# Grouping the tile shapes of a gated recurrence's score and output matmuls

## The reference, cut to what matters

```python
def chunk_gated_recurrence(q, k, v, log_f):
    C = HGRN_CHUNK                       # 64
    ...
    b = jnp.cumsum(lf, axis=-2)
    b_mid = b[..., C // 2:C // 2 + 1, :]
    scores = jnp.einsum('nbhtk,nbhsk->nbhts', q * jnp.exp(b - b_mid), k * jnp.exp(b_mid - b))
    o_intra = jnp.einsum('nbhts,nbhsv->nbhtv', jnp.where(causal, scores, 0.0), v)
    q_inter = q * jnp.exp(b)
    k_state = k * jnp.exp(b_last - b)
    def step(state, xs):
        qi, ks, vc, dec = xs
        o = jnp.einsum('bhtk,bhkv->bhtv', qi, state)
        state = dec[..., None] * state + jnp.einsum('bhsk,bhsv->bhkv', ks, vc)
        return state, o
    ...
    o = o_intra + o_inter
```

## Time and profile before

| | value |
|---|---|
| median of three runs | 1926.18 us (1922.85 to 1926.97) |
| span of the profiled execution, first to last instruction | 1922.8 us (the page gives no other time for it) |
| PE busy | 1847.2 us, 96% of the span |
| DVE busy | 1548.3 us, 81% |
| ACT busy | 1237.2 us, 64% |
| mean DMA rate | 256 GB/s |
| mean granted TensorE clock | 0.983 of full |

### The profile page before, as it was taken

How to read it: one execution, slowest core, us unless ns; L and a number is a source line. 1 busy time by engine, 2 the same in 40 slices (tenths; PEclk the granted TensorE clock), 3 DMA queues, 4 the chain that set the end, 5 groups by cost and what they waited for, 6 DMA issues and landing times.

```text
span 1922.8 us, 26965 instructions
## 1 busy us (share of the span) xinstructions
PE 1847.2 (96%) x9968; PEld 1576.8 (82%) x9968; DVE 1548.3 (81%) x1597; ACT 1237.2 (64%) x1280; POOL 1.4 (0%) x6
## 2 busy tenths in 40 slices
PE   7888999998899999999899999999999999999998
PEld 7777899887689988876788888888878888788886
DVE  8965788476567755665999998999989899898997
ACT  6966655366544435553577776777767777677776
POOL 0000000000000000000000000000000000000000
PEclk9999999999899999999899999999999999999999
DMA  9422455543135554433499998999989999899995
GB/s 369 148 88 88 162 189 176 197 154 110 66 142 187 178 195 154 140 117 127 177 380 361 356 376 323 373 364 362 382 313 366 370 369 373 330 355 375 350 377 207
DMA packets 68369, 491.48 MB, mean 256 GB/s; under 512 B 7712, under 2 KB 8096, under 8 KB 8992
## 3 DMA queue, kind: packets, MB, share of 16 engines
q1 hardware_dynamic: 67968, 488.52, 67.3%
q0 software_dynamic: 288, 1.31, 0.2%
HBM read 488.75 MB, written 1.05 MB: 255 GB/s over the span
## 4 chain that ended last, share of the span: by engine, by line
PE 84%; DVE 8%; ACT 5%; issue 2%; DMA 0%; SPq 0%; DVEq 0%; ACTq 0%
PE ps L419 25%; PE ps L428 19%; PE ps L421 19%; PE ps L430 6%; PE ps L423 6%; DVE wl L3076 1%; DVE wl L2126 1%; PE ps L439 1%; ACT wh L1423 1%; PE ps L1242 1%; PE ps L1340 1%; PE ps L1061 1%; DVE hTl L2184 1%; PE ps L1098 1%; PE ps L834 1%
## 5 line engine op out<-in xcount | busy, mean ns | idle before, releaser
L3076 DVE TENSOR_TENSOR wl<-raw,wh 128x2048 fp32r<-128x2048 f32 x336 | 760.9, 2288 | 57.4 <-ACT wh L2060 52.5
L2060 ACT ACTIVATE wh<-raw 128x2048 fp32r<-128x2048 f32 x336 | 644.3, 1919 | 205.9 <-PE ps L428 205.9
L419 PE MATMUL ps<-wh,hTh 128*128 128x512 f32 (+2 forms) x1128 | 444.5, 395 | 10.6 <-issue 5.1
L421 PE MATMUL ps<-wh,hTl 128*128 128x512 f32 (+2 forms) x1128 | 435.5, 387 | 0.0
L2126 DVE TENSOR_TENSOR wl<-raw,wh 128x2048 fp32r<-128x2048 f32 x124 | 283.6, 2290 | 125.0 <-ACT wh L1423 124.7
L1423 ACT ACTIVATE wh<-raw 128x2048 fp32r<-128x2048 f32 x125 | 238.5, 1913 | 138.1 <-PE ps L428 70.2
L428 PE MATMUL ps<-wl,hTh 128*128 128x512 f32 (+2 forms) x1128 | 301.4, 386 | 0.0
L419 PEld LDWEIGHTS ps<-wh,hTh 128*128 128x128 f32 x1128 | 212.7, 189 | 55.5 <-issue 11.0
L419 PE MATMUL ps<-wh,work_r 128*128 128x512 f32 x648 | 255.2, 394 | 0.4 <-DVE work_r L3081 0.4
L421 PE MATMUL ps<-wh,work_r 128*128 128x512 f32 x648 | 253.0, 390 | 0.0
L421 PEld LDWEIGHTS ps<-wh,hTl 128*128 128x128 f32 x1128 | 212.8, 189 | 40.2
(11 more groups left out here) (430 smaller groups left out, 1634.4 us busy)
## 6 DMA issues: line engine op xcount, KB each, us to landing
raw<-in_units SPq DMA_DIRECT2D x461, 1024.0 KB, 7.1
x<-in_x SPq DMA_DIRECT2D x2, 512.0 KB, 5.0
work<-in_lru_w SPq DMA_DIRECT2D x1, 1024.0 KB, 14.5
xn<-in_mem SPq DMA_DIRECT2D x1, 1024.0 KB, 17.5
out<-x SPq DMA_DIRECT2D x2, 512.0 KB, 3.1
consts<-in_consts POOLq DMA_DIRECT2D x1, 768.0 KB, 4.5
xn<-in_moe_gain POOLq DMA_DIRECT2D x1, 512.0 KB, 5.8
consts<-in_consts SPq DMA_DIRECT2D x1, 352.0 KB, 10.9
```

The source lines that it names most:

```text
L419: nc.tensor.matmul(out, sh, mh, start=(first and j == 0), stop=False)
L421: nc.tensor.matmul(out, sl, mh, start=False, stop=False)
L2060: A(wh[:, n % SPLIT, :], raw[:, n % RAW, :], ACT.Copy).then_inc(sem("hi_made"), 1)
L3076: V.tensor_tensor(wl[:, n % SPLIT, :], raw[:, n % RAW, :], wh[:, n % SPLIT, :].bitcast(F32), ALU.subtract).then_inc(sem("lo_made"), 1)
```

## The change

Nothing is computed otherwise; only the order of calls, two waits and the start flags differ. In `hg_scores` the loop over the two shapes is now the outermost: eight calls of 32 columns, then eight of 64. In `hg_out_of` the four score products come first and then the four state products, and the two waits for the state products stand between the two groups. Since two heads share a bank, only the first of them clears it (`start=(h % 2 == 0)`).

```diff
-            for h in (2 * pair, 2 * pair + 1):
-                for c in range(4):
-                    q0 = 64 * (c % 2)
-                    for m, lo in ((32, 0), (64, 32)):
+            for m, lo in ((32, 0), (64, 32)):
+                for h in (2 * pair, 2 * pair + 1):
+                    for c in range(4):
+                        q0 = 64 * (c % 2)
                         col0 = h * P + (c // 2) * 64 + lo
                         ins = nc.tensor.matmul(ps[q0:q0 + m, 4, col0:col0 + 32], gK[:, h, c * 64:c * 64 + m],
                                                gQ[:, h, c * 64 + lo:c * 64 + lo + 32], start=True, stop=True)
...
+            o = [ps[q0:q0 + 64, 6 + h // 2, (h % 2) * S + t * P:(h % 2) * S + (t + 1) * P] for h in range(4)]
+            for h in range(4):
+                ins = nc.tensor.matmul(o[h], AT[q0:q0 + 64, h, t * 64:(t + 1) * 64], gv[half][q0:q0 + 64, t, h * P:(h + 1) * P],
+                                       start=(h % 2 == 0), stop=(c == 0), skip_group_check=True)
             if c > 0:
                 pe.wait_ge(*reached("hgrn_factors", 4 * half + 3))
                 pe.wait_ge(*reached("hgrn_state", 3 * half + c))
-            for h in range(4):
-                o = ps[q0:q0 + 64, 6 + h // 2, (h % 2) * S + t * P:(h % 2) * S + (t + 1) * P]
-                ins = nc.tensor.matmul(o, AT[q0:q0 + 64, h, t * 64:(t + 1) * 64], gv[half][q0:q0 + 64, t, h * P:(h + 1) * P],
-                                       start=True, stop=(c == 0))
-                if c > 0:
-                    ins = nc.tensor.matmul(o, gq[:, 4 * half + h, c * 64:(c + 1) * 64], state[(c - 1) % 2][:, h, :], start=False,
-                                           stop=True)
+                for h in range(4):
+                    ins = nc.tensor.matmul(o[h], gq[:, 4 * half + h, c * 64:(c + 1) * 64], state[(c - 1) % 2][:, h, :],
+                                           start=False, stop=True, skip_group_check=True)
             counted(ins, "hgrn_o")
```

## The result

The changed kernel's first four executions took 1909.63 us in the median (1909.35 to 1916.81), against 1924.62 for the kernel before (1922.85 to 1926.97, four executions); the ratio is 0.9927 with a 95% interval of 0.9912 to 0.9942. Two later measurements of the same changed kernel gave 1913.88 and 1914.05 us, ratios 0.9943 [0.9925, 0.9960] and 0.9936 [0.9923, 0.9948].

A forecast was written before the change was run, and what follows sets the result against it. PE was taken to bound the recurrence layer; stretches capped by two waits gave 3.5 + 0.84 + 3.4 + 2.5 = 10.3 us, so 1926.18 - 10.3 = 1915.9 us. The range was 1911.8 to 1921.3 us.

The forecast's parts named there:

- PE alone sets the layer's pace: Recurrence layer, 785 to 886 us: PE always busy, so a microsecond off PE shortens the layer unless its suppliers become late.
- Output groups: Six mixed groups in chunks 1 to 3: each takes 2.04 us instead of 2.88, 0.84 saved, 5.0 us together.
- the rival in which loads don't hide: Weight loads can't hide in the same rows: output groups 2.34 us, score groups save 1.02, time 1918.9; chance 0.09.
- Score groups: Four groups: each takes 1.57 us instead of 3.28, 1.71 saved, 6.8 us together (4.1 to 11.5) before waits.
- a group below 1.4: Score-group sign of a wrong forecast: columns 0 and 64 run side by side; time would not change, only waits grow.
- The caps: Mask wait before L1073 limits one stretch to 3.4 to 3.5 us, L2867 wait before L1112 another to 3.4.
- The clock: Projection behind the first score group ran mostly at 1.2 GHz; shorter groups should end this, 1.5 us, mostly lost to the mask wait.
- The four terms: Layer stretches: to L1073 3.5, half 0 chunk 1 0.84, chunk 2 to L1112 3.4, half 1 2.5; sum 10.3 us.
- the rival for slower: Layer: two new waits idle PE and shifted work makes the clock fall more often, 1930 us; chance 0.02.
- Going on through the experts: Behind the layer: DMAs idle from 910 to 920 us, so the experts move whole and the gain counts in full.
- I take the sum from the median: 1926.18 - 10.3: Last step, whole program: the layer's 10.3 us taken from the runs' median gives 1915.9 us.
- a lower end set by the spread of three runs: Range's lower end, 1911.8 us: the forecast less the runs' spread of 4 us.

The follow-up runs named there:

- one-side run: Changed kernel with four score calls in a row writing output partitions 0 to 63, then four writing 64 to 127; ratio 0.9952 to the kernel before.
- the outputs alone: Kernel before with only the output groups' calls grouped by shape, old score loop kept; 1921.78 us, ratio 0.9978.
- the swaps alone: Kernel before with two swaps in DVE's list, first mask and second output-norm step each ahead of a weight conversion; 1925.38 us, ratio 0.9999.
- both repeats: Changed kernel measured again twice with no edit; 1913.88 us, ratio 0.9943, and 1914.05 us, ratio 0.9936.
- the kernel before against itself: Kernel before, no edit, measured against itself; 1925.79 us against 1925.34, ratio 1.0006.
- the score groups alone: Kernel before with only the score groups' calls grouped by shape, old output loop kept; 1917.93 us, ratio 0.9959.
- one shape: Kernel before in its old score order, both pieces of a chunk given the second's shape, output not the reference's; one execution, 1915.45 us.

## Why the prediction was off

- **PE alone sets the layer's pace.** Right: the layer's length in the experiments is PE's work plus the waits named.
- **Output groups.** Right: 2.03 us against the forecast 2.04, so the rival in which loads don't hide (2.34) falls.
- **Score groups.** Mis-sized: 1.71 us saved was forecast, 2.32 measured. The term took the distances of weight loads one after the other, 0.028 and 0.055 us, and within one side they are that: 0.032 and 0.058 between the starts in the one-side run. What it left out is that the calls for output partitions 0 and 64 run side by side once their shape is the same; the prediction named a group below 1.4 as the sign of that. With one side at a time the group is 1.37, and even there the records at the turn between the sides overlap. It did not move the sum, since both waits cap it, as the prediction said for higher savings; they grew instead, to 2.88 us before L1112 where 1.7 was forecast.
- **The caps.** Right. From the first score group to the second half of L1073 the changed kernel takes 791.86 - 780.93 = 10.93 us, 3.55 less than the 14.48 of before (forecast 3.5). From chunk 2's group in half 0 to L1112 it takes 839.43 - 810.78 = 28.65, 3.44 less than the 32.09 of before (forecast 3.4). The stretch between these two, with chunk 1's group, gave 0.88 (forecast 0.84) and the one behind L1112 2.49 (forecast 2.5). The four terms give 10.3, and the layer was 10.36 us shorter.
- **The clock.** Half right. The fall behind the first score group is in the four profiles with groups of 3.28 us and a layer at full work (the kernel before twice, the outputs alone, the swaps alone), and in none of the seven with shorter groups. How many of the four groups it follows varies with nothing changed in them: one in three of these profiles, three with the outputs alone. And in both repeats of the changed kernel a fall stands behind the new wait at L1073 and costs 1.3 to 1.4 us, in the one-side run behind the wait at L1112. That a wait may bring the clock down was in the rival for slower; here it happened inside the forecast.
- **Going on through the experts.** Right: the piece behind the layer is 1026.55 us against 1027.24, and 1026.26 and 1025.38 in the repeats; the kernel before against itself gave 1026.70. That it was some 0.9 us shorter on average shows nothing: over all eleven profiles this piece runs from 1025.38 to 1029.68 us (the longest with the score groups alone).
- **The step that failed** is the last one, "I take the sum from the median: 1926.18 - 10.3", with a lower end set by the spread of three runs. It put the change of the rest of the program at nothing and let it vary by 4 us. In the two profiles the part ahead of the layer, with the same instructions, took 780.93 us instead of 786.48; without these 5.55 us the median would have lain in the range. They come from PE's busy time (729.17 instead of 735.36), with a clock that was at half for 30.7 us instead of 47.8.

  Over the eleven profiles this part ran from 780.93 to 787.16 us. How long the clock is at half doesn't fix it alone: the eight with 44.4 us took 783.02 to 786.08. It goes with the places of the falls too: the four that have them at the same places (the kernel before again, both repeats, one shape) lie within 0.8 us, 783.02 to 783.82. Why three of the first four executions of the changed kernel had the highest clock stays open. Its eleven later executions had a median of 1913.88, inside the range.

  So the size from the profile, 10.4 us in the layer (9.0 where the clock fell in it), was right, and the miss of the first median is no sign of another mechanism in the layer. The repeats' ratios stand for 11.0 and 12.3 us, with intervals that reach down to 7.7 and 10.0. Whether the 2 to 3 us beyond their layers' 9.0 are real stays open.
- **A reading that did no harm.** The prediction calls the median 3.4 us above the execution that its sum was made on. It compared a time with a span; the span of that execution is always some us shorter than its time.

## What to carry to other kernels

Read a stream of small matmuls by the distance from start to start: where it is long at each change of tile shape, group the calls by shape, and let neighbours of one shape go to different output partitions. Before counting the gain, add up how much of it fits before each wait of that engine; what exceeds the slack turns into idle time, and the producer's list is then the place to work. Compare two profiles between two marks in the program and not by their spans, and take the noise of the rest from several executions.

## What the runs showed of the hardware

- A change of array shape between plain float32 calls cost about 0.09 us between 64\*64 and 128\*64 (0.20 against the 0.11 of a stream). In a score group of the old order they were more than half of the time (3.28 us against 1.37 grouped, one side at a time, where the records at the turns overlap a little too).
- Matmuls of one shape whose outputs lie in partitions 0 to 63 and 64 to 127 run side by side. The changed kernel's PE timeline, cut at one moment (781.20) in the 32-column part, lists the records that touch it:

```profile
781.01 0.36 PE L1061 MATMUL ps<-work 128*32 128x32 f32 x12
```

  The ends of matmul records are modelled, so twelve at one moment doesn't mean twelve in the array; the starts tell more. A record is 0.20 us long, so these twelve start (0.36 - 0.20) / 11 = 0.015 us apart on average, by the trace 0.007 and 0.025 in turns. With one side at a time they start 0.031 to 0.032 apart. So each side keeps its own pace, and the second side costs hardly anything beside the first.
- The Trainium skill, "TensorE: Matmul & The Clock Gate", Part 3, The mechanism, lets a weight load overlap a running matmul only where the row group differs. L1101, which uses all 128 rows, took 1.01 us for eight records, 0.11 apart inside the group, so its loads hid in one row group; the trace disagrees with that rule. The same page's statement, in the section "Why this matters for your kernels", that small matmuls whose outputs go to distinct column groups run concurrently agrees with the 0.96 us against 1.37 with one side at a time.
